# Softmax attention's scores from high and low parts in one-pass matmuls, with x parked in DRAM to make room

## The reference, cut to what matters

```python
ss = jnp.einsum('bghqd,bgqnld->bghqnl', q_pos, ks, preferred_element_type=jnp.float32)
p_s = masked_softmax(ss, m_s)
o_s = jnp.einsum('bghqm,bgqmd->bghqd', p_s.astype(vs.dtype), vs)
sw = jnp.einsum('bghqd,bgkd->bghqk', q_pos, kwin, preferred_element_type=jnp.float32)
p_w = masked_softmax(sw, m_w)
o_w = jnp.einsum('bghqk,bgkd->bghqd', p_w.astype(vwin.dtype), vwin)
return gt[..., 0:1] * o_c + gt[..., 1:2] * o_s + gt[..., 2:3] * o_w
```

## Time and profile before

| | us |
|---|---|
| median of 3 runs (1422.94 to 1424.19) | 1424.11 |
| the profiled execution | 1432.34 |
| its span, first to last instruction | 1430.4 |
| PE busy in it | 1410.3 |
| DVE busy | 786.3 |
| ACT busy | 539.2 |
| POOL busy | 171.8 |

### The profile page before, as it was taken

The page is one execution under the profiler, slowest core; times in us unless marked ns, Lnnn a source line. Parts: engine busy times, 40 slices in busy tenths (PEclk is TensorE's granted clock), DMA queues, the critical chain, the costliest instruction groups (busy, mean ns, idle before and its releaser), DMA issues.

```text
span 1430.4 us, 17436 instructions
## 1 busy us (share of the span) xinstructions
PE 1410.3 (99%) x7191; PEld 1145.7 (80%) x7191; DVE 786.3 (55%) x1130; ACT 539.2 (38%) x772; POOL 171.8 (12%) x163
## 2 busy tenths in 40 slices
PE   6999999999999999999999999999999999999998
PEld 5888788988888888888878776668888888888887
DVE  4999764654334343368374567774545545434433
ACT  5222343643323232255453437662343223212214
POOL 3040004100000000120031712111210000000002
PEclk8999999999999999999999999999999999999999
DMA  7223223313223223322334222112322332232221
GB/s 196 89 89 118 73 88 108 115 36 113 89 88 115 92 89 116 98 89 76 108 74 134 72 60 60 30 31 60 114 92 89 90 117 89 90 115 90 88 88 60
DMA packets 136015, 129.67 MB, mean 91 GB/s; under 512 B 15777, under 2 KB 131425, under 8 KB 135905
## 3 DMA queue, kind: packets, MB, share of 16 engines
q1 hardware_dynamic: 134800, 124.90, 28.2%
q0 software_dynamic: 992, 3.47, 0.8%
q10 hardware_dynamic: 144, 0.20, 0.0%
HBM read 126.06 MB, written 2.10 MB: 90 GB/s over the span
## 4 chain that ended last, share of the span: by engine, by line
PE 95%; ACT 1%; DVE 1%; POOL 1%; DMA 1%; issue 1%; SPq 0%; ACTq 0%
PE gemm L467 75%; PE gemm L575 3%; PE gemm L958 2%; PE misc L979 2%; PE misc L998 1%; PE gemm L659 1%; PE gemm L606 1%; PE gemm L1039 1%; POOL w_lo L2378 1%; PE gemm L971 1%; PE misc L807 1%; DMA w_raw<-in_w_in 1%; PE misc L606 1%; PE misc L971 1%; PE gemm L1072 1%
## 5 line engine op out<-in xcount | busy, mean ns | idle before, releaser
L1682 DVE TENSOR_TENSOR w_lo<-w_raw,w_hi 128x2048 fp32r<-128x2048 f32 (+1 forms) x108 | 245.9, 2277 | 176.1 <-ACT w_hi L1135 174.7
L467 PE MATMUL gemm<-h_hi,w_hi 128*128 128x512 f32 x828 | 325.0, 393 | 0.0
L467 PE MATMUL gemm<-h_hi,w_lo 128*128 128x512 f32 x828 | 322.4, 389 | 0.0
L467 PE MATMUL gemm<-h_lo,w_hi 128*128 128x512 f32 x828 | 322.3, 389 | 0.0
L1135 ACT ACTIVATE w_hi<-w_raw 128x2048 fp32r<-128x2048 f32 (+1 forms) x113 | 214.0, 1894 | 143.9 <-PE gemm L467 139.5
L467 PEld LDWEIGHTS gemm<-h_hi,w_hi 128*128 128x128 f32 x828 | 155.5, 188 | 35.3 <-issue 2.4
L467 PEld LDWEIGHTS gemm<-h_hi,w_lo 128*128 128x128 f32 x828 | 155.4, 188 | 32.6
L467 PEld LDWEIGHTS gemm<-h_lo,w_hi 128*128 128x128 f32 x828 | 155.5, 188 | 32.2 <-issue 0.5
L467 PE MATMUL gemm<-n_hi,w_hi 128*128 128x512 f32 x336 | 130.9, 390 | 0.0
L467 PE MATMUL gemm<-n_lo,w_hi 128*128 128x512 f32 x336 | 130.7, 389 | 0.0
L467 PE MATMUL gemm<-n_hi,w_lo 128*128 128x512 f32 x336 | 130.7, 389 | 0.0
(11 more groups left out here) (469 smaller groups left out, 1955.9 us busy)
## 6 DMA issues: line engine op xcount, KB each, us to landing
w_raw<-in_w_in SPq DMA_DIRECT2D x62, 512.0 KB, 4.6
w_raw<-in_w_down SPq DMA_DIRECT2D x32, 512.0 KB, 4.1
w_raw<-in_w_up SPq DMA_DIRECT2D x28, 512.0 KB, 4.4
w_raw<-in_w_ffn_gate SPq DMA_DIRECT2D x22, 512.0 KB, 4.6
w_raw<-in_w_ffn_up SPq DMA_DIRECT2D x22, 512.0 KB, 4.5
w_raw<-in_w_ffn_down SPq DMA_DIRECT2D x16, 512.0 KB, 4.1
w_raw<-in_w_o SPq DMA_DIRECT2D x8, 512.0 KB, 4.1
w_raw<-in_w_out SPq DMA_DIRECT2D x8, 512.0 KB, 4.3
```

What stands on the lines that cost most here:

```text
L467: mm = nc.tensor.matmul(bank[:], w(s)[:, kt, col0:col0 + P], x(n), start=first, stop=last)
L1682: V.tensor_tensor(part(lo_of(s), s), part(raw_of(s), s), f(part(hi_of(s), s)), SUB).then_inc(S("lo_done"), SLABS_AT[s])
```

## The change

The scores are made from split operands. For each block of 128 queries a tile `q_scores` of group g holds, on the 64 rows of its own group, the high part of the queries, and on the other 64 rows their low part. `k_scores` of group g holds the high part of that group's keys on both halves, twice. One matmul over 128 rows then gives (q_hi + q_lo) * k_hi. A second one on 64 rows adds q_hi * k_lo, with `k_scores_low` written over `k_rope`. So a group's scores are two one-pass matmuls into one bank, and the two 64-row ones stand on different halves of the array. Two versions of `q_scores` take turns (t % 2).

The tiles take the 16 KB of `x_T`. x is stored to DRAM (`x_kept`) in four DMAs of 512 KB in SP's list behind the loads of four weight slabs, and read back in four, two of them ahead of `w_out`'s first slab. ACT waits for the stores before it writes the new tiles; DVE waits for the returns (`x_loaded`) before it adds to x.

```diff
+    QS = [at(f"q_scores{g}", [2, 4, P], f32r, 4 * g) for g in range(2)]
+    KS = [at(f"k_scores{g}", [2, T], f32r, 8 + 4 * g) for g in range(2)]
+    KLOW = at("k_scores_low", [2, T], f32r, R1 + 74)
+    KEPT = nc.dram_tensor("x_kept", [P, KT, T], f32).ap()
+    X_OUT_AT = (4, 5, 6, 7)
...
             load(s0 + 1 + j, halves(s0 + 1 + j, w_2, 0, c0))
+            if j in X_OUT_AT:
+                sp.wait_ge(S("x_ready"), 2 * KT)
+                ks = slice(2 * X_OUT_AT.index(j), 2 * X_OUT_AT.index(j) + 2)
+                sp.dma_start(KEPT[:, ks, :], XT[:, ks, :]).then_inc(S("stored"), 16)
...
-        run("wout", tiles(a["w_out_2"][0]))
+        def x_back(i):
+
+            sp.wait_ge(S("scores_full"), 2 * STEPS)
+            ks = slice(2 * i, 2 * i + 2)
+            sp.dma_start(XT[:, ks, :], KEPT[:, ks, :]).then_inc(S(f"x_loaded{i}"), 16)
+
+        x_back(0)
+        x_back(1)
+        for j in range(4):
+            s = PH["wout"][0] + j
+            load(s, halves(s, tiles(a["w_out_2"][0]), 0, SLAB * j))
+            if j < 2:
+                x_back(2 + j)
...
             if step >= 2:
                 pe.wait_ge(S("exp_done"), 2 * step - 2)
+            if step % 8 == 0:
+                pe.wait_ge(S("heads_split"), 3 + t)
+            for g in range(2):
+                nc.tensor.matmul(banks[g][:, 0:w + P], QS[g][:, t % 2, q, :], KS[g][:, i, 0:w + P], start=True, stop=False)
             for g in range(2):
                 rows = slice(64 * g, 64 * g + 64)
-                nc.tensor.matmul(banks[g][:, 0:w + P], QT[rows, q, w:w + P], KR[rows, i, 0:w + P],
-                                 start=True, stop=True).then_inc(S("scores_full"), 1)
+                nc.tensor.matmul(banks[g][:, 0:w + P], QS[g][rows, t % 2, q, :], KLOW[rows, i, 0:w + P],
+                                 start=False, stop=True).then_inc(S("scores_full"), 1)
...
         A_(HT[:], M[2][:, 0:P], ACT.Tanh, scale=0.5).then_inc(S("hidden_tanh"), 1)
+        act.wait_ge(S("stored"), 16 * 4)
+        for i in range(2):
+            act.wait_ge(S("ropes_ready"), i + 1)
+            for g in range(2):
+                for to in range(2):
+                    ins = A_(KS[g][64 * to:64 * to + 64, i, :], KR[64 * g:64 * g + 64, i, :], ACT.Copy)
+            ins.then_inc(S("heads_hi"), 1)
+
+        def q_hi(t):
+
+            act.wait_ge(S("ropes_ready"), 6)
+            if t >= 2:
+                act.wait_ge(S("scores_full"), 2 * 8 * (t - 1))
+            for g in range(2):
+                rows = slice(64 * g, 64 * g + 64)
+                ins = A_(QS[g][rows, t % 2, :, :], QT[rows, :, t * P:(t + 1) * P], ACT.Copy)
+            ins.then_inc(S("heads_hi"), 1)
+
         act.wait_ge(S("hidden_T"), 1)
         A_(HXT[:].rearrange("p k n -> p (k n)"), M[3][:, 0:P], ACT.Copy).then_inc(read[3], 1)
+        q_hi(0)
...
             if step + 2 < STEPS:
                 probs(step + 2)
+            if step % 8 == 1 and step // 8 + 1 < TT:
+                q_hi(step // 8 + 1)
...
         rope(4)
         rope(5)
+        def k_lo(i):
+
+            dve.wait_ge(S("heads_hi"), i + 1)
+            for g in range(2):
+                rows = slice(64 * g, 64 * g + 64)
+                ins = V.tensor_tensor(KLOW[rows, i, :], KR[rows, i, :], f(KS[g][rows, i, :]), SUB)
+            ins.then_inc(S("heads_split"), 1)
+
+        def q_lo(t):
+
+            dve.wait_ge(S("heads_hi"), 3 + t)
+            for g in range(2):
+                rows, others = slice(64 * g, 64 * g + 64), slice(64 - 64 * g, 128 - 64 * g)
+                ins = V.tensor_tensor(QS[g][others, t % 2, :, :], QT[rows, :, t * P:(t + 1) * P], f(QS[g][rows, t % 2, :, :]), SUB)
+            ins.then_inc(S("heads_split"), 1)
+
+        k_lo(0)
...
+        k_lo(1)
...
         split(16)
+        q_lo(0)
...
             if s + 2 < STEPS:
                 row_max(s + 2)
+            if s % 8 == 2 and s // 8 + 1 < TT:
+                q_lo(s // 8 + 1)
...
                 split_lo(s0 + k // 2 + 1)
+                dve.wait_ge(S(f"x_loaded{k // 2}"), 32)
```

More of the change, by code:

```diff
@@ L451, in _ @@
                              OTK[:, t, side * T:(side + 1) * T]).then_inc(S("stored"), 16)
-        sp.wait_ge(S("stored"), 16 * 2 * TT)
+        sp.wait_ge(S("stored"), 16 * (4 + 2 * TT))
     @block.tensor
@@ L2054, in _ @@
         dve.wait_ge(read[1], 1)
-        V.tensor_scalar(GATES[:], GTH[:], 0.5, 0.5, MUL, ADD).then_inc(S("gates_ready"), 1)
+        V.tensor_scalar(GATES[:], GTH[:], 0.5, 0.5, MUL, ADD)
         dve.wait_ge(S("masks_small"), 1)
@@ L2290, in _ @@
         fbase = H2 + 2 * KT
-        fstep = Count(S("ffn_step"))
+        fstep = step
         def gate_up(name, ch):
```

## The result

The changed kernel takes 1432.6 us (median of 6 runs, 1429.5 to 1435.5) against 1424.1 for the kernel before (6 runs, 1422.9 to 1425.7): a ratio of 1.006, 95% interval 1.005 to 1.007. It is slower by 8.5 us. The forecast was 1423.0 with a range up to 1426.6, so forecast and range are both wrong, and in sign.

What follows compares the result with a forecast made beforehand. The prediction took PE's own instruction list as the bound (busy 1410.3 of 1430.4 us). With 3.2 us saved on scores and 2.1 lost in waits, 1.1 less, the median of 1424.11 would become 1423.0, range 1420.3 to 1426.6.

Steps and rivals of the forecast that it cites:

- `q_lo(1)` and `q_lo(2)`, 0.6 + 0.4: DVE's low query parts at steps 2 and 10 delay copies; PE waits 0.6 and 0.4 us at the values.
- `q_hi(3)`, 1.1: ACT's two high query copies at step 17 delay the scaling of step 19; PE waits 1.1 us.
- `q_hi(1)` and `q_hi(2)`: ACT's earlier high query copies inside the steps: taken as covered, 1.1 us each if not.
- The matmuls, 3.2 saved: Scores on PE: 0.19, 0.15 and 0.06 us less per step at 512, 384 and 256 keys, eight steps each.
- a fixed 0.21: Scores on PE: the 64-row pair costs this many us besides one stream, put down to weight load and drain.
- The work before the steps, nothing: ACT's key copies and DVE's subtractions before the steps fit into idle time, at no cost.
- DMA, nothing: Four stores and four returns of x, 512 KB each, stay hidden: cost 0, or 4.6 us per transfer waited for.
- rival 1: Slack in the steps takes the late copies, so PE has no waits: 1420.5 us, chance 0.16.
- Pair taking turns: The two 64-row score passes run one after the other, 5.1 us more per run: 1428.1 us, chance 0.09.
- Narrow passes four times as long: One-pass score matmuls at 128 columns stream four times as long, 1.9 us more: 1424.9 us, chance 0.10.
- Weights of the second pass loading alone: Each second full-height score pass comes a weight load later, 3.5 us more: 1426.5 us, chance 0.04.
- The transfer: PE waits for one store or return of x, 4.6 us: 1427.6 us, chance 0.04.

Runs made afterwards that it cites:

- experiment 1: The changed kernel without the in-loop q_hi and q_lo, every step taking the first block's split queries: 1422.45 us, ratio 0.9994; its attention takes 109.5 us.
- Experiment 9: The changed kernel with each q_lo two steps later, where POOL has finished its low weight parts: 1427.44 us, ratio 1.0021.
- experiment 7: The kernel of experiment 4 with q_hi(3) and q_lo(3) put back where the changed kernel has them: 1424.16 us.
- experiment 4: The changed kernel with all query splits kept but moved to before the steps or to steps with slack: 1422.68 us, ratio 0.9987.
- experiment 3: The changed kernel with the gate matmuls ahead of the second transpose in steps 3 and 11: 1428.53 us, ratio 1.0028.
- experiment 10: The changed kernel with q_lo taken off DVE and put on POOL, behind its low weight parts: 1424.82 us, ratio 1.0008.
- experiment 2: The kernel before with only three pairs of 64x512 DVE subtractions added, at steps 2, 10 and 18: 1434.35 us, ratio 1.0071.

## Why the prediction was wrong

The loss of the profiled execution, against the 109.5 us of experiment 1: PE waited 2.2 us in step 3 and 2.2 in step 11, 1.4 went at step 18 to 19, and 5.4 to the half clock (3.5 in steps 4 to 6, 0.7 in step 12, and 0.6 each in steps 3 and 11 beyond their waits). That is 11.3, less the 1.5 that the matmuls bring, so 9.8 on the attention. The medians differ by 8.5 and not by 9.8, for the profiled execution was 1.5 above the median of its kernel.

- **The step that failed: `q_lo(1)` and `q_lo(2)`, 0.6 + 0.4.** Measured 2.2 + 2.2, with three causes. (a) The place: the margin was taken at the values, but the second transpose waits for DVE's copy of the first through their common bank, and has hardly any margin at that point. In the kernel before, the copy of step 3 ended at 862.79 and the second transpose started 0.15 later:

```profile
862.94 0.30 PE L979 MATMUL misc<-ident,probs 128*128 128x128 f32 x1
```

  Experiment 9 prices this alone, two steps further on: 0.77 to 0.93 a pair, with each pair at 1.38. (b) The size of the pair: 1.3 was taken from instructions that met nothing on POOL; beside `w_lo` it is 2.42 and 2.28 in the change's trace, and experiment 9 shows that POOL is the reason. The trace of before had shown it on an instruction I had not read for it, DVE's factor: 0.16 while POOL stood idle, 0.68 while it was at its low parts:

```profile
880.68 0.16 DVE L2243 TENSOR_TENSOR o_factor<-o_factor,gates 128x2 f32<-128x2 f32 x1
...
884.39 0.68 DVE L2243 TENSOR_TENSOR o_factor<-o_factor,gates 128x2 f32<-128x2 f32 x1
...
882.53 4.99 POOL L2504 TENSOR_TENSOR w_lo<-w_raw,w_hi 128x512 fp32r<-128x512 f32 x4 [18.75 <-ACT w_hi L1135]
```

  The Trainium skill has this rule too (SBUF — State Buffer, section Who interferes with whom): a VectorE instruction with two SBUF inputs and a GpSimd instruction that reads SBUF shut each other out for a whole instruction. The runs agree: 0.69 alone, 1.66 and 1.58 beside POOL in the change. (In the other direction, POOL's last op of 850.84 took 1.71 where DVE had started first.) (c) The clock: no term had it, and at 5.4 us it is the largest part of what was missed.
- **`q_hi(3)`, 1.1**: right in place and mechanism, 1.4 in size (experiment 7). The two copies took 1.26, not 1.08: the 0.54 an op came from a tanh that reads a PSUM bank, while a copy from SBUF to fp32r takes 0.63 whether it has 64 partitions or 128 (`h_hi<-h_T`, L1143, in the kernel before). `q_hi(1)` and `q_hi(2)`, at nothing: right.
- **The matmuls, 3.2 saved**: 1.5 (experiment 1), with nothing saved in six of the eight steps with 256 keys. Entry with the first pass (0.34 at 512 keys, 0.33 predicted) and the second pass with the change of shape (0.33; 0.32 predicted) were right. The mis-sized term is the pair: from its starts to the next transpose 0.48 at 512 keys, 0.46 at 384, 0.44 at 256, where a fixed 0.21 and one stream gave 0.42, 0.37 and 0.32. Shorter streams buy almost nothing there; the floor seen at 128 keys (0.37) reaches much further up. What makes up the fixed 0.21, which the prediction put down to a weight load and a drain, no run shows.
- **The work before the steps, nothing**: right. The eight K copies took 0.62 to 0.64 each, more than the 0.54 priced, and still fit ACT's idle time. **DMA, nothing**: right; no wait names a transfer, and experiment 1 has all of them in it.
- **The rivals.** No waits (rival 1, 1420.5) is what experiments 1 and 4 bring about, at 1422.5 and 1422.7. Pair taking turns: false, the L997 starts are 3 to 4 ns apart. Narrow passes four times as long: false, the 128-key step has the predicted 0.80, as before. Weights of the second pass loading alone: false, it follows 0.31 behind the first at 512 keys, as the second L958 behind the transpose does in the earlier trace rows (941.74 to 942.05). So the Trainium skill's "only" on row groups, which the prediction cites, doesn't hold for these full-height passes; the section cited there (TensorE: Matmul & The Clock Gate, The mechanism) itself also names loads into a background weight buffer. The transfer: false. None of them foresaw the loss, and it lay outside the range for a cost that neither the forecast nor a rival had.
- My test "PE's waits over 3.5 us" did catch it: they are 6.2 at the transposes with the step 19 wait, and 7.2 with those at the values (1.0 in all before the change).

What stays open: why the clock fell behind the 0.88 and 0.52 us of step 11 in experiment 3 and not behind the 1.57 us of experiment 7, and why it stayed down for 10 us behind one wait of 2.2 us and for 3.4 behind the other four. The mean clock varies between executions of one kernel, the one before too (0.995 to 0.999); what decides it no run shows. The split of 5.4 us is for the profiled execution alone.

## What to carry to other kernels

Price a late instruction at every place that waits for it, buffers included: here the first reader in line was not the consumer of the data but the next writer of the same bank. Before adding work to VectorE, read what GpSimd does at that time, and look for an ordinary instruction of the trace that has already met it. And on a kernel whose TensorE is 99% busy a wait of 2.2 us can cost more than its length, here 6.3 and 3.5 us with the half clock behind it. Small pieces where an engine waits anyway (experiment 4) turn the same change from 8.5 us lost into 1.4 won; moving only DVE's part to an idle engine (experiment 10) brings it back to no measurable difference.

## What was not expected of the hardware

- Behind all five waits of 2.1 to 2.2 us in two traces (the change and experiment 2) the granted clock went to 0.50, for 10 us of fully busy PE once and for 3.4 four times. Behind 1.6 us it stayed at 1.00 at step 19 in all six traces that have this wait. It also fell where PE waited for nothing: nine of the twelve traces have 3.4 or 6.8 us at 0.50 in front of step 0, begun during or after 64 matmuls of 31 columns.
- A DVE subtraction of two SBUF operands of 64x512 takes 0.69 us alone. One that starts while a POOL subtraction runs takes 0.74 to 1.69, the longer the more of POOL's is left, and each ends 0.55 after POOL's instruction; POOL's own was stretched from 1.28 to 1.71 where DVE had started first.
- One-pass matmuls on 64 rows run side by side like the fp32 ones (starts 3 to 4 ns apart), but a pair keeps the next full-height matmul at least 0.37 us away at 128 columns and only 0.48 at 512.
